# Output projection and state updates of a small hybrid model interleaved by steps of 128 rows, and two bias loads moved

## What is computed

```python
def token_mixers(...):
    ...
    out = jnp.concatenate([o_gdn, o_gla], axis=-1).astype(h.dtype) @ w_out      # 1024 x 1024
    return (out, conv_new..., s_gdn_new..., s_gla_new...)

def moe(x2d, w_router, b_router, w_up, b_up, w_down, b_down):
    logits = x2d @ w_router + b_router
    top_v, top_i = lax.top_k(logits, TOP_K)
    gates = jax.nn.softmax(top_v, axis=-1)
    ...
    def expert_block(args):
        xe, e = args
        gu = xe @ w_up[e] + b_up[e]                                              # 1024 -> 2048
        gate = jnp.minimum(gu[:, :D_FF], SWIGLU_LIMIT)
        up = jnp.clip(gu[:, D_FF:], -SWIGLU_LIMIT, SWIGLU_LIMIT)
        act = (up + 1.0) * gate * jax.nn.sigmoid(SWIGLU_ALPHA * gate)
        return act @ w_down[e] + b_down[e]
    ...
    out = jnp.zeros((n_tok + 1, d)).at[row_tok].add(yb * row_gate[:, None])

def trunk(x, ...):
    x = x + mix
    x = x + moe(rmsnorm(x, rms_ffn_w[l]), ...)
    return rmsnorm(x, rms_final_w), ...
```

## Time and profile before

| what | value |
|---|---|
| runs | 1256.35, 1251.3, 1247.83 us; median 1251.3 |
| the profiled execution | 1255.04 us |
| its span | 1253.0 us |
| TensorE busy | 1216.4 us (97%) |
| VectorE, ScalarE, GpSimd busy | 379.9, 215.1, 73.3 us |
| mean granted clock of TensorE | 0.989 |
| HBM | 428.39 MB read, 4.88 MB written, 346 GB/s over the span |
| chain that ended last, by engine | TensorE 78%, DMA 15%, VectorE 4% |

### The profile page before, as it was taken

One profiled execution on the slowest core, in us unless ns is written; L12 is line 12 of the kernel. 1 busy time (PEld: TensorE's weight loads), 2 busy tenths in 40 slices (PEclk: granted clock), 3 DMA queues, 4 the chain that ended last, 5 costly groups with the idle time before them and its releaser, 6 DMA issues.

```text
span 1253.0 us, 15623 instructions
## 1 busy us (share of the span) xinstructions
PE 1216.4 (97%) x6225; PEld 590.7 (47%) x6225; DVE 379.9 (30%) x802; ACT 215.1 (17%) x522; POOL 73.3 (6%) x116
## 2 busy tenths in 40 slices
PE   6999999899999999999999999999999999999996
PEld 5777787766443434343343434343333424242432
DVE  3685774552222121213032121213031221212123
ACT  2143333323110101011110101011111201010102
POOL 5010103241000000000000000000000000000000
PEclk9998999889999999999999999999999999999999
DMA  9422110279899999999999999999999999999994
GB/s 272 131 83 99 40 68 2 73 276 366 313 383 420 419 430 426 428 427 429 430 427 429 427 429 429 428 428 428 430 428 428 428 428 430 428 428 428 428 430 190
DMA packets 49805, 433.75 MB, mean 346 GB/s; under 512 B 7422, under 2 KB 13898, under 8 KB 25196
## 3 DMA queue, kind: packets, MB, share of 16 engines
q1 hardware_dynamic: 48588, 429.46, 82.8%
q0 software_dynamic: 1184, 3.84, 1.1%
HBM read 428.39 MB, written 4.88 MB: 346 GB/s over the span
## 4 chain that ended last, share of the span: by engine, by line
PE 78%; DMA 15%; DVE 4%; ACT 1%; issue 1%; POOL 0%; SPq 0%; DVEq 0%; POOLq 0%; ACTq 0%
PE bank L986 31%; PE bank L1005 13%; DMA ring<-in_w_up 11%; PE bank L962 7%; PE bank L1014 5%; PE bank L599 4%; PE bank L536 3%; DMA ring<-in_w_down 3%; PE bank L691 3%; PE bank L970 2%; PE bank L860 2%; DMA hT<-in_b_up 1%; PE bank L748 1%; PE bank L757 1%; PE bank L844 1%; PE bank L755 1%
## 5 line engine op out<-in xcount | busy, mean ns | idle before, releaser
L986 PE MATMUL bank<-ring,xb 128*64 128x512 f32 x2048 | 448.5, 594 | 7.0 <-DMA ring<-in_w_up 5.8
L986 PEld LDWEIGHTS bank<-ring,xb 128*64 128x64 f32 x2048 | 144.1, 137 | 306.8 <-issue 295.8
L1005 PE MATMUL bank<-ring,qkv 128*64 128x512 f32 x1024 | 227.2, 595 | 2.1 <-DMA ring<-in_w_down 1.4
L1506 DVE TENSOR_TENSOR qkv<-qkv,bank 128x512 f32<-128x512 f32 (+1 forms) x102 | 69.7, 683 | 270.4 <-PE bank L962 270.4
L1005 PEld LDWEIGHTS bank<-ring,qkv 128*64 128x64 f32 x1024 | 70.7, 137 | 134.3 <-issue 127.7
L962 PE MATMUL bank<-xb,bT 128*128 128x512 f32 (+1 forms) x204 | 97.1, 611 | 0.9 <-DVE xb L1498 0.9
L1014 PE MATMUL bank<-rowsel,ob 128*128 128x128 f32 x768 | 91.2, 275 | 0.5 <-DVE rowsel L1521 0.5
L1498 DVE COPY xb<-bank 64x512 f32<-64x512 f32 x16 | 11.1, 694 | 262.9 <-PE bank L1005 262.9
L1014 PEld LDWEIGHTS bank<-rowsel,ob 128*128 128x128 f32 x768 | 88.7, 192 | 2.0 <-issue 1.3
L1485 DVE TENSOR_SCALAR xb<-bank 128x512 f32<-128x512 f32 x32 | 21.8, 681 | 197.5 <-PE bank L536 176.6
L599 PE MATMUL bank<-hT,ring 128*128 128x288 f32 x320 | 81.6, 416 | 0.0
(11 more groups left out here) (345 smaller groups left out, 884.6 us busy)
## 6 DMA issues: line engine op xcount, KB each, us to landing
ring<-in_w_up SPq DMA_DIRECT2D x128, 2048.0 KB, 23.6
ring<-in_w_down SPq DMA_DIRECT2D x64, 2048.0 KB, 26.5
ring<-in_w_in SPq DMA_DIRECT2D x7, 2048.0 KB, 8.2
ring<-in_w_out SPq DMA_DIRECT2D x2, 2048.0 KB, 8.5
ring<-in_state_gdn SPq DMA_DIRECT2D x4, 512.0 KB, 10.5
out<-ring POOLq DMA_DIRECT2D x1, 2048.0 KB, 15.2
xb<-in_x_prompt SPq DMA_DIRECT2D x1, 1024.0 KB, 5.6
sls<-in_state_gla SPq DMA_DIRECT2D x4, 256.0 KB, 7.2
```

Of the source, the lines that this page charges most:

```text
L986: last = pe.matmul(bank[2 * q + g][CAP * h:CAP * (h + 1), :], xeT[:, at, q * CAP:(q + 1) * CAP], w[:, kk, g, h, :], start=False, stop=at = ...
L1005: last = pe.matmul(bank[5 - q][CAP * h:CAP * (h + 1), :], aTs[q][:, kk, CAP * u:CAP * (u + 1)], w[:, kk, h, :], start=u == 0 and kk == 0, ...
L1506: v.tensor_tensor(d, d, bank[banks[at]][0:TN[t], :], ALU.add).then_inc(sems["sc_ok"], 1)
```

## The change

**The projection.** `state_update(h)` becomes `state_b(h, b)`, one sequence of an update, and `mixed(t, j)` becomes `mix_k(t, j, k)`, one step of 128 rows; `logits` becomes `logit(t, m)`. TensorE now runs one or a few small matmuls behind each step of a large half. The order of halves becomes (0,0), (0,1), (1,0) with (2,0) beside it, (1,1) with (2,1) beside it. Update 0 runs in (0,0), updates 1 and 2 in (0,1), update 3 in (1,0), update 4 and the logits of tile 0 in (1,1), update 5 before the routing counts. PSUM banks and the orders of VectorE, ScalarE and GpSimd follow. Six short filler matmuls are added before the output of the chunks, and four of 512 columns before the first gather become one.

**Loads.** The up bias has a buffer of its own and is loaded right after the residual rows, ahead of load 0. Load 4 waits for projection tick 33 instead of 34. SyncE loads `b_down` where it loaded the up bias.

**The down bias.** The first turn has no scatter any more. The turned gates stay in `sm`, and the last turn scatters the down bias in `bias_scatter` behind its own scatter, with VectorE adding six more half tiles.

**The first gather.** Its banks change, and the first expert starts when the first two of four copies are done.

```diff
-        b_gu = hTf[:, 0:512]
+        b_gu = sb("b_gu", [P, 512])
+        b_dn = hTf[:, 0:D]
...
+            for j in range(4):
+                sp.dma_start(b_gu[E_N * j:E_N * (j + 1)], a["b_up"][0, :, 512 * j:512 * (j + 1)]).then_inc(sems["ld_bias"], 16)
...
-            sp.wait_ge(sems["p_proj"], 34)
+            sp.wait_ge(sems["p_proj"], 33)
             load_unit(0, 4, 0)
...
+            sp.dma_start(b_dn[0:E_N], a["b_down"][0]).then_inc(sems["ld_down"], 16)
...
+            seq_rows(4)
...
             g.wait_ge(sems["p_up_s"], 4)
-            g.wait_ge(sems["kdm_ok"], 4)
-            seq_rows(4)
+            g.wait_ge(sems["kdm_ok"], 5)
             seq_rows(5)
...
+            keep_busy(3, 6)
...
-            mixed(0, 0)
-            pe.wait_ge(sems["gch_ok"], 1)
+            pe.wait_ge(sems["oT_ok"], 2)
+            for k in range(KT):
+                mix_k(0, 0, k)
+                if k == 4:
+                    pe.wait_ge(sems["gch_ok"], 1)
+                    pe.wait_ge(sems["kdm_ok"], 1)
+                if k >= 4:
+                    state_b(0, 2 * k - 8)
+                    state_b(0, 2 * k - 7)
...
+            BESIDE = [[], [], [0], [1], [2], [3], [4, 5], [6, 7]]
+            for k in range(KT):
+                mix_k(1, 0, k)
+                if k == 2:
+                    pe.wait_ge(sems["oT_ok"], 6)
+                    pe.wait_ge(sems["st_ok"], 2)
+                    pe.wait_ge(sems["kdm_ok"], 4)
+                for n in BESIDE[k]:
+                    mix_k(2, 0, n)
+                    state_b(3, n)
...
-            keep_warm(5, 4)
+            keep_warm(2, 1)
...
+            def bias_scatter(w):
+
+                pe.wait_ge(sems["ld_down"], 16)
+                for at in range(6):
+                    t, j, b = BIAS_AT[at]
+                    if at in (2, 4, 5):
+                        pe.wait_ge(sems["sc_ok"], w * 6 + (1 if at == 2 else at))
+                    pe.matmul(bank[b][0:TN[t], :], sm[0:E_N, TO[t]:TO[t] + TN[t]], b_dn[0:E_N, 512 * j:512 * (j + 1)],
+                              start=True, stop=True).then_inc(sems["p_sc"], 1)
...
                 if not first:
-                    up(i, 1, k, odd)
+                    pe.wait_ge(sems["yb_ok"], w * 4 + 4)
+                    pe.wait_ge(sems["S_ok"], i + 2)
+                    scatter(w)
+                if last:
+                    bias_scatter(i)
+                    pe.wait_ge(sems["sc_ok"], i * 6 + 3)
+                up(i, 1, k, odd)
```

276 lines of the change are left out of this document (145 added, 131 removed).

## The result

Timed side by side, the kernel before took 1253.8 us (median of 4; 1247.8 to 1258.8) and the changed one 1272.0 (median of 4; 1267.8 to 1274.9): a ratio of 1.0158, 95% interval 1.0121 to 1.0195. Slow executions, over 1.5% above the fastest of their kernel, are left out of every ratio; only e6 has any (two of ten). The profiled execution of the changed kernel took 1274.86 with a span of 1272.5 and a mean granted clock of 0.978; that of before 1255.04, 1253.0 and 0.989. The forecast was 1252.0, its range 1245.5 to 1258.5.

The account below looks back on a forecast made before the run. From about 370 us DMA bytes set the end. Load 3's trigger 2.2 later, 7.9 earlier by closed holes and moved up bias, 3.6 later by last-turn scatter: 1255.04 becomes 1252.9, lowered to 1252; range 1245.5 to 1258.5.

Parts of the forecast that it names:

- the price of interleaving: Projection on TensorE: alternating large and small matmuls costs nothing; bounds minus 1.2 to plus 1 us.
- 33.1 to the trigger: Projection: from its start to load 3's trigger, halves, updates, turning and waits at full clock sum to 33.1 us.
- 63 to the first expert: TensorE from the projection's start to the first expert: 63 us instead of 70.6, so the expert starts at 310.5.
- The path: Weight stream: DMA full from load 3's trigger to the end, load 8 asked for at 314, well before 322.
- The baseline of the trigger: Load 3's trigger: 28.4 us after the projection's start before; 4.7 later in the new order if the start stays.
- Then the projection starts at 247.4: Before the projection: fillers keep the clock from falling, so it starts 2.5 us earlier (bounds 0 and 3.0).
- Load 4, load 5 and the state output: SyncE's queue: load 4 goes with load 3's trigger, load 5 about 19.2 us after it, at 299.7.
- 7.9 earlier by the rest: Weight stream: closed DMA holes (7.3 us) and the up bias moved out (0.6) bring the last load 7.9 us earlier.
- The bias scatter in the last turn: Last turn on TensorE: 5.3 us of scatter less 1.7 slack makes the end 3.6 us later (bounds 0 and 4.0).
- Rival 2: End follows the first expert's start, not DMA holes: 9.9 us earlier, plus 3.6 for the bias, 1248.7; chance 0.15.
- Rival 3: Slower: clock falls as before, load 3's trigger at 286.4, 8.1 us later, end 1258.8; decides beyond 282.6; chance 0.18.
- Rivals 1 and 4: 1: last turn hides the bias scatter, 1249.3 us (0.12); 4: DMA idles more at load 5, up to 1256 (0.10).

Follow-up runs that it names:

- e6: Kernel before with only the two bias edits (early up bias, down bias scattered in the last turn): 1251.5 us, ratio 0.9989.
- e2: Changed kernel with the same order, but each half and each update as one whole block, not alternating: 1253.2 us, ratio 0.9998.
- e1: The changed kernel run and profiled once more, unaltered: 1266.5 us, ratio 1.0111 to the kernel before.
- e10: Kernel before with the two bias edits, bias scatter padded with zeros to 128 rows: 1248.4 us, ratio 0.9955.
- e12: Changed kernel with whole blocks instead of alternating steps, and the bias scatter padded to 128 rows: 1250.4 us, ratio 0.9975.
- e3: Changed kernel in whole blocks, with update 3 and the sample half ahead of the large half (1,0): 1257.9 us, ratio 1.0046.
- e11: Kernel before with only the six short filler matmuls added: 1251.7 us, ratio 0.9985.
- e9: Changed kernel with 32-row operands of updates 0 to 3 read as 128 rows, zero-filled on VectorE at the start: 1276.4 us, ratio 1.0153.
- e8: Changed kernel, last turn's bias scatter reading the ordinary scatter's 128-row operands (output leaves out the down bias): 1260.6 us, ratio 1.0054.
- e4: Changed kernel with the down bias scattered in the first turn again, still reading 32 rows: 1265.8 us, ratio 1.0085.

## Why the prediction was wrong

**The step that failed: the price of interleaving.** "Interleaving itself hides at most some small weight loads; I price it at nothing (bounds: minus 1.2, all updates limited by columns alone, to plus 1, a weight load exposed at every change of kind)." The exposed load was named, but bounded too low: it costs 0.3 us a step, 7.2 us up to load 3 (39.3 against e2's 32.2) and 11.0 up to load 8 (77.0 against 66.0 without the falls). The sums of whole pieces were right: 33.1 to the trigger, and e2 has 32.2; 63 to the first expert and 3.6 on to load 8, and e2 has 66.0. At equal clock the alternation costs 10.7 us in the end (1258.7 against 1248.0), the same size.

**The path, wrong as well.** "I expect DMA to be full from the trigger to the end": the prediction carried the trigger of load 3 straight to the end and took load 8 to be asked for at 314, "well before 322". It went at 341.6 (e1 327.0), and the end follows it, not the trigger: against e10, e12 has its trigger 7.0 us later after A, but load 8 only 3.8 later, and C 3.4. The 3.8 is less than half of its 13.7 us at 0.50. In e3 the trigger came 6.4 earlier than in e2 and gained nothing.

**The baseline of the trigger.** The 28.4 us of before held a clock fall, as the prediction said; but it counted the fall's undoing as a gain of the change. In e6, e10 and e11, which keep the old order, the fall was absent and A to B 25.2. Against that the trigger is later by 14.1 and not by 4.7. Half of this, 7.0, is the new order of the halves, half the alternation.

**"Then the projection starts at 247.4."** Near for e1 (246.6) and most experiments, wrong for the profiled execution (257.8), and luck in both: the start is 242.4 to 243.6 us plus half of the time at 0.50 ahead of it in every profile but e9, with the fillers or without. They gained nothing that a run shows, where the prediction counted 2.5.

**Load 4, load 5 and the state output.** Right: loads 3 and 4 went together, load 5 18.8 us behind (forecast 19.2). It did not decide the end.

**The stream.** Of "7.9 earlier by the rest" 5.1 came for certain: load 8 to C is 867.2 us instead of 872.3, by the scatter that left the first turn. The rest hung on an earlier first expert. C was 12.3 us later in the profile: load 8 17.4 later, less the 5.1.

**The bias scatter in the last turn, mis-sized.** 3.6 us was what full clock gives (e10: 60.3 - 56.6 = 3.7, the slack of 1.7 included). Missing was a further 3.4 us: the clock falls behind matmuls of 32 rows, and the scatter itself, the bias row and the second expert all get longer. Bounds of 0 and 4.0 did not allow for it. The gain of the first turn (5.1) no longer covers the loss in the last turn (7.1).

**The sum, from before's profile to those of the changed kernel.** Start of the projection: forecast 2.5 earlier, 3.3 earlier in e1 and 7.8 later in the first profile. From there to load 8: 6.2 and 9.6 later. Load 8 to C: 5.1 less in both. Last turn: 7.1 more in both (forecast 3.6). Together 4.9 and 19.4 later; the spans differ by 4.8 and 19.5. What lies between e1's profile, its fastest execution, and its median is the clock.

**The rivals.** Rival 2, that the end follows the first expert's start, is the path that the traces show; the DMA share of 1.00 held against it is that of the stream behind load 8 and says nothing about when load 8 goes. Its price was wrong, since the first expert started not 9.9 us earlier but 2.8 (e1) and 17.4 later. Rival 3 had the direction right, slower, and not the reason: there was no clock fall in the updates up to load 3, but exposed weight loads, and they count on the way to the first expert. Its point, a trigger later than 282.6, does not decide: e3's came at 277.2, and its span was 1260.9. Rivals 1 and 4 did not occur.

The passage on the Trainium skill's rule of the clock stood as the rows had it. In the last turn too the rule that the clock follows how busy TensorE is decides nothing: in e6 and e10 TensorE was busy all through the scatter (6.00 of 6.00 us, 5.60 of 5.60), and the clock behind it was 0.50 and 1.00.

## What to carry to other kernels

Before alternating two kinds of matmuls, look at the weight-load queue where the kinds already meet once: the idle time before the first load shows that every further change will cost something, and here the operands of 32 rows paid it. Filling up with zeros cost nothing where another engine had the time (GpSimd in e10 and e12; in e9 the fills stood first on VectorE, and the projection started 23 us later than in e1), and it also held the clock. To find what sets the end, look for the mark from which the distance to the end is the same in all versions: here it was load 8 and not load 3. And before you price a fall of the clock as a gain, look whether it is in most executions or only in the profiled one: the span against the mean clock of all runs tells that.

## What was not expected of the hardware

- Weights of 32 rows are not loaded ahead of running matmuls of 128 rows (e1: 0.76 us of idle load queue, 0.3 us a step); weights of 128 rows are (e9: loaded at 280.14, used at 280.57; 1.31 us a step instead of 1.69).
- Twelve passes of 32 rows by 512 columns were followed by a granted clock of 0.50, the level of 1.2 GHz (e6; the mean over 1196 to 1206 is 0.66); the same with 128 rows by 1.00, that of 2.4 GHz (e10; e8 with other values in the rows). Worth 3.4 us of 1250. In the first turn too: 0.50 behind 32 rows (e4), 1.00 behind 128 (before).
- A mean granted clock that is lower by 0.001 is 1.06 us more of span in the kernel before (91 executions), and 0.96 to 1.22 in the others with ten runs or more.
